# First layer of a four-layer fp32 model on one core: rows transposed between the tiles of the first projection block, retention worked off chunk by chunk between the tiles of the last four blocks

## The reference

```python
hn = rmsnorm(h, norm_gain[i])                       # rows of x
z = einsum('bsd,df->bsf', hn, w_in)                 # 1024 x 4096
qa, ka, va, ga, qb, kb, vb, gb = split(z, 8)        # 512 columns each
o_a = retention(qa, ka, va, ret_gn_gain)            # 4 heads of 128, chunks of 128 rows
o_b = stick_breaking(qb, kb, vb)                    # 4 heads of 128
mixed = concat([o_a * silu(ga), o_b * silu(gb)])
h = h + mixed @ w_out

# retention, for chunk n: q, k rotated by cos and sin of the position
scores = (qc @ kc.T) * intra
out = scores @ vc + (qc * qdec) @ state             # state: what the chunks before left
state = state * chunk_decay + (kc * kdec).T @ vc
o_a = head_norm(out) * gn_gain
```

## Time and profile before

| | us |
|---|---|
| median of 3 runs | 4376.22 |
| lowest, highest run | 4370.87, 4381.23 |
| the profiled execution | 4367.83 |
| its span | 4366.0 |
| PE busy in the span | 3796.1 (87%) |
| DVE busy | 2018.5 (46%) |
| ACT busy | 1699.4 (39%) |
| POOL busy | 103.8 (2%) |

### The profile page before, as it was taken

How to read it: one execution, slowest core, us unless ns; L and a number is a source line. 1 busy time by engine, 2 the same in 40 slices (tenths; PEclk the granted TensorE clock), 3 DMA queues, 4 the chain that set the end, 5 groups by cost and what they waited for, 6 DMA issues and landing times. The chain is left out here.

```text
span 4366.0 us, 48176 instructions
## 1 busy us (share of the span) xinstructions
PE 3796.1 (87%) x18874; PEld 3067.0 (70%) x18874; DVE 2018.5 (46%) x3947; ACT 1699.4 (39%) x3121; POOL 103.8 (2%) x120
## 2 busy tenths in 40 slices
PE   5998567998999599999789799999878999998789
PEld 4886533766887477777677677777766688887666
DVE  2111723235332567667524355555554355555442
ACT  3211156144342234333314344444433455555420
POOL 0000221000000000000000000000000000000000
PEclk9999778998999577777899899999978999999789
DMA  2222120221222111211222111011032011110310
GB/s 103 103 87 106 56 79 0 78 92 53 106 83 94 46 51 42 51 45 49 83 78 77 42 30 30 25 30 30 26 111 73 36 57 39 34 35 15 125 54 39
DMA packets 214841, 261.16 MB, mean 60 GB/s; under 512 B 62556, under 2 KB 138452, under 8 KB 213592
## 3 DMA queue, kind: packets, MB, share of 16 engines
q1 hardware_dynamic: 214616, 258.08, 18.0%
HBM read 189.60 MB, written 68.42 MB: 59 GB/s over the span
## 5 line engine op out<-in xcount | busy, mean ns | idle before, releaser
L301 PE MATMUL bank<-wh,XH 128*128 128x512 f32 x1344 | 556.1, 414 | 53.5 <-DVE wl L285 36.1
L301 PE MATMUL bank<-wl,XH 128*128 128x512 f32 x1344 | 532.1, 396 | 0.0
L301 PE MATMUL bank<-wh,XL 128*128 128x512 f32 x1344 | 531.6, 396 | 0.0
L2220 PE MATMUL bank<-XH,wh 128*128 128x512 f32 x1040 | 427.6, 411 | 32.0 <-DVE wl L2209 19.7
L2220 PE MATMUL bank<-XH,wl 128*128 128x512 f32 x1040 | 412.4, 397 | 0.0
L2220 PE MATMUL bank<-XL,wh 128*128 128x512 f32 x1040 | 411.6, 396 | 0.0
L301 PEld LDWEIGHTS bank<-wh,XH 128*128 128x128 f32 x1344 | 257.0, 191 | 125.3 <-issue 50.7
L285 DVE TENSOR_TENSOR wl<-raw,wh 128x1024 fp32r<-128x1024 f32 x128 | 153.9, 1224 | 407.8 <-ACT wh L279 406.6
L301 PEld LDWEIGHTS bank<-wh,XL 128*128 128x128 f32 x1344 | 256.9, 191 | 63.4 <-issue 10.3
L301 PEld LDWEIGHTS bank<-wl,XH 128*128 128x128 f32 x1344 | 256.0, 190 | 57.9
L301 PE MATMUL bank<-XH,wh 128*128 128x512 f32 x704 | 278.4, 395 | 6.0 <-DVE XL L1330 6.0
(11 more groups left out here) (398 smaller groups left out, 7314.3 us busy)
## 6 DMA issues: line engine op xcount, KB each, us to landing
sc_zt<-stage SPq DMA_DIRECT2D x88, 256.0 KB, 2.0
raw<-in_att_w_in SPq DMA_DIRECT2D x33, 512.0 KB, 4.2
raw<-in_even_w_in SPq DMA_DIRECT2D x32, 512.0 KB, 4.8
raw<-in_odd_w_in SPq DMA_DIRECT2D x32, 512.0 KB, 4.7
raw<-in_rec_w_in SPq DMA_DIRECT2D x32, 512.0 KB, 4.0
sc_h<-H SPq DMA_DIRECT2D x24, 512.0 KB, 2.6
H<-sc_h SPq DMA_DIRECT2D x24, 512.0 KB, 8.1
sc_z<-stage SPq DMA_DIRECT2D x40, 256.0 KB, 2.0
```

Of the source, the lines that this page charges most:

```text
L301: done = e.matmul(out, lhsT, rhs, start=k == 0 and j == 0, stop=k == NK - 1 and j == 2)
L2220: done = e.matmul(bank[:, :], x[:, k, :], y[:, k, ts], start=k == 0 and j == 0, stop=k == NK - 1 and j == 2)
```

## The change: what it does, and the diff

- `Start` is gone. `EvenIn` now carries one list, `plan`, that gives the order of all work for all engines: entries that stand in front of tile t, then tile t. Rows 0 and 1 are transposed ahead of it, row s (2 to 7) in front of tile s - 2, the squares of rows 3, 4 in front of tile 1 and of rows 5 to 7 in front of tile 3. The parts of the first weight block stand between rows 0, 1 and 2; those of block i + 1 in front of tiles 2 to 5 of block i.
- Tiles use two PSUM banks in turn (4 and 5) in place of eight; banks 0 to 3 take the transposes, then retention's.
- `Retention` has no phase of its own. Chunk n is read in front of tile 26 + 4n, rotated at 29 + 4n, transposed at 30 + 4n, scored at 31 + 4n, summed and normalized at 32 + 4n, and its result transposed at 34 + 4n.
- q is multiplied by its decay ahead of the matmul (`qd`, a table `qrow` in place of `qdec`), so both parts of the output accumulate in one bank; ScalarE copies it out. Most buffers exist once, z twice.
- The result goes to DRAM (rows 2048 to 2559 of `zt`) in place of `XH`, `XL`; `Stick` reads it back as `kept` and splits it on VectorE (`ve_kept`) four times, between its parts 1 and 2 at key blocks 5 to 2 of the first half.
- `Stick` does not wait for the last stores before its tables, q, k and v. SP reaches those loads after the last tile's store.

```diff
+    def plan(self):
+        order = [("sq", 0, 1), ("turn", 0), ("w", 0, 0), ("w", 0, 1), ("sq", 1, 3), ("turn", 1), ("w", 0, 2), ("w", 0, 3)]
+        front = {t: [] for t in range(64)}
+        for s in range(2, NS):
+            front[s - 2] += [("sq", *g) for g in self.GROUPS[2:] if g[0] == s] + [("turn", s)]
+        front[6] += [("features", 0)]
+        for t in range(56):
+            if 2 <= t % 8 <= 5:
+                front[t] += [("w", t // 8 + 1, t % 8 - 2)]
+        for n in range(NS):
+            for part, at in (("in", 26), ("rotate", 29), ("turn", 30), ("score", 31), ("sum", 32), ("out", 34)):
+                front[at + 4 * n] += [(part, n, "ret")]
+        for t in range(64):
+            order += front[t] + [("tile", t)]
+        return order
...
+    def sp(self, e, before, following):
...
+        for s in range(NS):
+            e.dma_start(self.rows[s][:, :], self.x[s * P:(s + 1) * P, :]).then_inc(*self.row[s].up())
+            if s == 0:
+                for q in range(3):
+                    self.w.load(e, q)
+            if s == 2:
+                self.w.load(e, 3)
...
+    def pe_tile(self, e, t):
+        i, j = t // 8, t % 8
+        if t >= 2:
+            f, k = self.out(t - 2)
+            e.wait_ge(*f.at(*k))
+        if i == 0:
+            wait_all(e, self.marks[j])
+        bank = self.c.banks[4 + t % 2]
...
+    def ac(self, e, before):
...
+            elif what == "sq":
+                for s in range(n, rest[0]):
...
+                    e.activation(self.sq[:, :], self.rows[s][:, :], ACT.Square, accum_out=self.st[:, s:s + 1]) \
+                        .then_inc(*self.squared.up(s))
+                e.wait_ge(*self.meant.at(n))
+                e.activation(self.st[:, n:rest[0]], self.st[:, n:rest[0]], ACT.Sqrt).then_inc(*self.rooted.up(n))
...
+            elif what == "tile":
+                e.wait_ge(*self.tile.at(n // 8, n % 8))
+                if n >= 4:
+                    e.wait_ge(*self.sent[n % 4].at(n - 4))
+                fn = ACT.Sigmoid if self.blocks[n // 8][2] else ACT.Copy
+                e.activation(self.stage[n % 4][:, :], c.banks[4 + n % 2][:, :], fn).then_inc(*self.copied.up(n))
...
 class Retention:
...
+    def pe(self, e, part, n):
...
+        if part == "turn":
+            e.wait_ge(*self.rotated.at(n))
...
+        elif part == "sum":
+            e.wait_ge(*self.masked.at(n))
+            if n:
+                e.wait_ge(*self.ocopied.at(n - 1))
+                e.wait_ge(*self.qdec.at(n))
+                e.wait_ge(*self.stated.at(n - 1))
+            for h in range(4):
+                if n:
+                    e.matmul(c.banks[3][:, hs(h)], self.qd[:, hs(h)], self.state[:, h, :], start=True, stop=False)
+                done = e.matmul(c.banks[3][:, hs(h)], self.sc[:, hs(h)], v[:, h, :], start=n == 0, stop=True)
+            done.then_inc(*self.summed.up(n))
...
+        elif part == "sum":
+            e.wait_ge(*self.summed.at(n))
+            if n:
+                e.wait_ge(*self.norm.at(n - 1))
+            e.activation(self.o[:, :], c.banks[3][:, :], ACT.Copy).then_inc(*self.ocopied.up(n))
+            e.wait_ge(*self.norm.at("var", n))
+            e.activation(self.mv[:, :, 1], self.mv[:, :, 1], ACT.Sqrt).then_inc(*self.rooted.up(n))
...
+    def po(self, e, n):
...
+        e.wait_ge(*self.zin[n % 2].at(n))
+        if n:
+            e.wait_ge(*self.rotated.at(n - 1))
+        e.tensor_tensor(B[:, :, 0, :], qk[:, :, 1, :], sin, ALU.mult)
+        e.tensor_tensor(B[:, :, 1, :], qk[:, :, 0, :], sin, ALU.mult).then_inc(*self.sines.up(n))
+        if n:
+            e.wait_ge(*self.gated.at(n - 1))
+        e.tensor_tensor(self.sg[:, :], z[:, 1536:2048], self.gn[:, :], ALU.mult).then_inc(*self.gains.up(n))
...
 class Stick:
...
     def sp(self, e, before):
-        wait_all(e, before)
+        wait_all(e, self.even_in.ret.read)
+        wait_all(e, [(self.even_in.sent[u % 4], (u,)) for u in range(52, 56)])
...
+        wait_all(e, before)
+        for h in range(4):
+            e.dma_start(self.kept[h][:, :], self.zt[2048 + h * P:2048 + (h + 1) * P, :]).then_inc(*self.keptin[h].up())
...
+    def ve_kept(self, e, h):
+        c = self.c
+        e.wait_ge(*self.keptin[h].at())
+        e.tensor_copy(c.XH[:, h, :], self.kept[h][:, :]).then_inc(*self.keph.up(h))
+        e.wait_ge(*self.keph.at(h))
+        e.tensor_tensor(c.XL[:, h, :], self.kept[h][:, :], f32(c.XH[:, h, :]), ALU.subtract).then_inc(*self.kepl.up(h))
...
+                if half == 1 and h == 3 and 2 <= kb <= 5:
+                    self.ve_kept(e, 5 - kb)
```

More of the change, by code:

```diff
@@ L302, in product @@
     return done
[L305 to L387, removed]
@@ L756, in po @@
         pass
[L759 to L767, removed]
-                                   for blk, mode, at in order], 4)
-        self.w = Weights(c, column_blocks(w_in), self.project.tile, 7, ahead=0)
-        self.marks, self.ends = self.start.marks, [(self.project.tile, (7, 7)), *self.project.stored]
-    def sp(self, e, before, following):
-        self.start.sp(e)
-        self.features.sp(e)
-        self.w.sp(e, 0)
-        sp_blocks(e, self.project, self.w, 8)
-        following.first(e)
-    def pe(self, e, before):
-        self.start.pe(e)
-        self.features.pe(e)
-        free = [[(self.start.low, (6 + j // 2, j % 2))] if j < 4 else [] for j in range(7)] + [[(self.features.copied, ())]]
-        pe_blocks(e, self.project, self.w, 8, [self.marks[j] + free[j] for j in range(8)])
-    def ac(self, e, before):
-        self.start.ac(e, self.w)
-        ac_blocks(e, self.project, self.w, 8)
-    def ve(self, e, before):
-        self.start.ve(e, self.w)
-        self.features.ve(e)
-        ve_blocks(e, self.project, self.w, 8)
-    def po(self, e, before):
-        pass
 def seq_rows(z, at):
@@ L904, in pe @@
                 for h in range(4):
[L905 to L906 removed]
+                    done = e.transpose(c.banks[j][:, hs(h)], self.A[:, 512 * j + P * h:512 * j + P * (h + 1)], c.ident[:, :])
+                done.then_inc(*self.turned.up(n, j))
+        elif part == "score":
+            e.wait_ge(*self.qk.at(n, 1))
+            if n:
+                e.wait_ge(*self.masked.at(n - 1))
+            for h in range(4):
+                done = e.matmul(c.banks[2][:, hs(h)], k(h), q(h), start=True, stop=True)
+            done.then_inc(*self.scored.up(n))
+            if n < NS - 1:
+                e.wait_ge(*self.decayed.at(n))
@@ L907, in pe @@
                 if n:
-                    for h in range(4):
-                        done = e.matmul(c.banks[4][:, hs(h)], q(h), self.state[:, h, :], start=True, stop=True)
-                    done.then_inc(*self.inter.up(n))
-                e.wait_ge(*self.decayed.at(n))
+                    e.wait_ge(*self.stated.at(n - 1))
                 for h in range(4):
-                    done = e.matmul(c.banks[5][:, hs(h)], self.heads(self.kd, n)[:, h, :], v[:, h, :], start=True, stop=True)
+                    done = e.matmul(c.banks[6][:, hs(h)], self.heads(self.kd)[:, h, :], v[:, h, :], start=True, stop=True)
@@ L914, in pe @@
                 done.then_inc(*self.kv.up(n))
-                e.wait_ge(*self.masked.at(n))
-                for h in range(4):
-                    done = e.matmul(c.banks[3][:, hs(h)], self.sc[n % 3][:, hs(h)], v[:, h, :], start=True, stop=True)
-                done.then_inc(*self.summed.up(n))
-            elif part == 3:
-                e.wait_ge(*self.gated.at(n))
-                for h in range(4):
-                    done = e.transpose(c.banks[6 + n % 2][:, hs(h)], self.y[n % 3][:, hs(h)], c.ident[:, :])
-                done.then_inc(*self.yturned.up(n))
@@ L3203, in program @@
         c.without_x()
-        both = [ret.marks[s] + stick.marks[s] for s in range(NS)]
         def sync(e):
             even_in.sp(e, [], end0.w)
-            ret.sp(e, even_in.ends)
-            stick.sp(e, ret.ends)
+            stick.sp(e, even_in.ends)
             end0.sp(e, stick.ends, odd_in)
```

442 lines of the change are left out of this document (279 added, 163 removed).

## The result

The changed kernel takes 4253.64 us (median of 4 runs, 4247.65 to 4270.02) against 4378.54 for the kernel before on the same chip (4 runs, 4370.87 to 4381.23): ratio 0.9723, 95% interval 0.9693 to 0.9754, faster by 124.9 us. The profiled execution took 4255.36, its span is 4253.6. The forecast was 4282 with a range of 4258 to 4318: direction and mechanism hold, the gain came out larger than the range allows.

The account below looks back on a forecast made before the run. Engine chains around a PE-bound product were taken as the bound. 30.2 + 359.0 + 19.7 + 37.4 + 4 + 11.6 gave stick-breaking's start at 461.9, not 557.70; less 1, a gain of 94.8 us: 4282, range 4258 to 4318.

Parts of the forecast that it names:

- The bound: Before stick-breaking: chains over several engines bind 60.65 us ahead of the product and 138.05 behind; PE alone binds the product.
- The start: Rows ahead of the product: first tile begins at 30.2 in place of 60.65; net gain about 10.8 us.
- Rival (c): Start doesn't come forward, through late weights or longer stops for squares: price 10.8 us, time about 4292, chance 0.05.
- What the product pays: Rows between the first tiles: two PE stops of 5.2 and 6.4 us, restarts, transposes and features, 19.7 us in all.
- Retention between the tiles: Eight chunks put 37.4 us of PE work into the product's stream, plus 4 us of waits for even chunks' rotations.
- Rival (b): Retention's chain stays in part, PE waiting in most chunks: price up to 43 us, time 4300 to 4325, chance 0.16.
- rival (d): Stops between the last 32 tiles pull PE to the 1.2 GHz level: slower, up to 4461, chance 0.04.
- Fewer banks, SP's queue: In the product, two tile banks and the reads and stores moved onto SP cost 0.
- The pause: Between the last tile and stick-breaking's first matmul PE pauses 11.6 us, as SP loads only behind the last store.
- Stick-breaking: Reading retention's result back and splitting it on DVE four times adds 1 us, bounds 0 and 9.6.
- 359.0: The product's 64 tiles by themselves take 359.0 us, as in the kernel before.
- (a): The forecast itself: 4266 to 4300, with 0 to 20 us of waits in place of 4; chance 0.74.

Follow-up runs that it names:

- The second series of the changed kernel: The changed kernel measured once more, unaltered, on one chip beside the kernel before: 4263.44 us (5 runs), ratio to before 0.9770.
- the kernel with both edits: Changed kernel with squares of rows 3 to 7 earlier and stick-breaking's loads ahead of tile 61's store: 4240.28 us, second time 4236.88.
- the earlier squares: Changed kernel with squares of rows 3, 4 ahead of tile 0 and of rows 5 to 7 ahead of tile 1: 4251.29 us.
- before with 128 bytes: Kernel before with tile `st` taking 128 bytes a partition in place of 32, moving the first projection's weights: 4376.64 us (one run).
- the one with the loads alone: Changed kernel with stick-breaking's tables and q, k, v of heads 0 to 2 issued ahead of tile 61's store: 4244.3 us.

## Why the prediction was right, and where it wasn't

**The bound** was named rightly. All the gain to stick-breaking's first matmul, 557.70 - 447.39 = 110.3 us (forecast 95.8), comes from the two stretches in which PE idled and from the pitch; what lies behind it changed by 2.1 us in sum.

**The start** held: 29.22 for 30.2, stops of 6.7 and 8.2 us with 11.1 of idle time for a forecast 11.6, and 10.2 net by the run that put the rows in front. Rival (c) falls.

**"What the product pays"** held in its sum. The transposes behind the first stop took 1.75, not 1.97.

**Retention between the tiles** held in its main term: 37.7 counted by insertions, 38.8 by the run with the rows first, for 37.4. Its small term was sized too high. The text put 1 us on each even chunk, since POOL's gate product would fall on the rotation. It ends before:

```profile
259.88 1.30 POOL L1062 TENSOR_TENSOR sg<-z,gn 128x512 f32<-128x512 f32 x1 [10.07 <-DVE y L1140]
...
262.44 0.69 DVE L1087 TENSOR_TENSOR A<-z,cos 128x512 f32<-128x512 f32 x1
...
264.37 0.69 DVE L1092 TENSOR_TENSOR A<-A,B 128x512 f32<-128x512 f32 x1
...
265.40 1.04 PE L990 MATMUL bank<-ident,A 128*128 128x128 f32 x8
```

POOL is done at 261.2, the rotation starts behind it at the short 0.69, ends at 265.06, and PE comes at 265.40. Counted from the end of tile 35 (252.27) that is 12.8 for the rotation and 13.1 for PE, where the forecast had 13.5 and 13.4: right to 0.7 us, with the sign on the good side, by a margin of 0.3. Rival (b), which saw PE waiting in most chunks, falls: PE waited 0.4 us, once. What those waits cost when they do come, the run with retention behind the product shows: 109 us.

**The clock**, rival (d), falls too. In the last 33 tiles, with 24 insertions, the granted clock is 1.00:

```profile
218.00:435.88 217.88, 217.88 (x1126) 185.48 (x1125) 89.44 (x218) 53.41 (x87) 30.92 (x21) 1.00 0.35 117
```

With retention behind the product its stretch has 0.59:

```profile
399.81:556.50 156.69, 71.34 (x337) 62.88 (x337) 79.00 (x204) 22.64 (x42) 35.99 (x28) 0.59 0.26 85
```

The Trainium skill (TensorE: Matmul & The Clock Gate, section A second HAM failure mode: psum-queue depth-cycling) tells of a bf16 kernel that cycles through PSUM banks and whose TensorE idles for moments between groups of matmuls. Here the two banks brought no such idling, 217.88 of 217.88 us busy, and no lower clock; the forecast took the banks alone for the cause.

**Fewer banks, SP's queue** cost nothing, as said: no wait of PE for a copy. **The pause** held, 11.51 for 11.6. **Stick-breaking** grew by 3.2 us to its last `q`k matmul, more than the 1 of the forecast and just over the 3 us that it named as a sign of being wrong; 1.5 of them are left at LayerEnd's first matmul. The bounds 0 and 9.6 hold. Its length scatters: 179.3 to 184.5 us in four profiles with the code of before in this phase, 182.6 to 187.8 in seven with that of after, on the mean 181.6 and 185.9. So a growth is likely. Whether it comes from the four splits on DVE or from the heads' later arrival (0.8 us more to the ninth matmul), no run tells.

**The step that failed** is the first term of the sum, "359.0". It took the product's length from before as fixed, because its instructions stayed the same. Their operands didn't stay where they were: with `Start` gone, `st` no longer lies in front of the weights. That is worth 9.9 us (359.0 - 349.1), shown by taking it away from after (+9.6) and giving it to before (-9.6). The trace of before held a sign of it. The same instruction (L301) had a pitch of 0.2267 in the unbroken stretch from 1100 to 1400 us, and 0.2333 in the first product, at a granted clock of 1.00 in both.

In the span the miss is 4271.2 - 4253.6 = 17.6 us: 1.0 from the start, 9.9 from the pitch, 3.6 from waits that didn't come (the small differences of the other terms cancel), and 3.1 behind stick-breaking's first matmul, where the forecast had 1 more and the trace 2.1 less. These 3.1 are within what the later stages scatter by. In the median it is 28.4, and the rest isn't the change's: 8.4 us were added because before's profiled execution lay below its median, after's lay 1.7 above its own, so 10.1, and 0.6 was rounding. The second series of the changed kernel has 4263.44 as its median, within the range: that the number fell outside it the first time, 4.4 us below, is decided by the scatter, the wrong first term is not. The low end of 4258 allowed for 4 us of waits and the runs, and had no room for a term of the product itself. The chances have a slip: (a) to (c) with half of (d) make 0.97, not 0.96.

## What to carry to other kernels

- An edit that takes tiles out or adds them moves all that is allocated behind them. Before taking the length of an untouched stretch over, compare its pitch with that of the same instruction elsewhere in the trace, and list the operands' addresses of both kernels.
- A chain over several engines is hidden when its parts stand between tiles of a stretch that PE fills: the same parts behind it cost 109 us more. What PE itself does in them can be counted from rows of such insertions to within one or two microseconds.
- Look behind the first late thing: the order of squares on ACT (12.5 us of the product) and the loads of the later heads on SP (9.3 us) were worth more in the trace than the pause that stood in the chain of waits (3.3 us). And see whether such a gain reaches the end: in the whole time of one series the squares brought 4 us on top of the loads.

## What the runs showed of the hardware

- **Pitch and place.** A matmul of 512 columns, 128 by 128 stationary, has a pitch of 0.2267 us in an unbroken stretch when its two SBUF operands lie a multiple of 256 bytes apart in the partition, and 0.2333 at 32 bytes beside that, whichever of the two (activations or weights) is the stationary one, with a granted clock of 1.00 either way. At 64 bytes 0.2289 or 0.2333, at 128 bytes 0.2333 or 0.2323, by block. Other distances weren't run. The mechanism is open.
- **Identical stages scatter.** From the last `q`k matmul of stick-breaking to a matmul early in `Fox`, its first of weights times v (line 2568 of after), all kernels run the same code (the end of `Stick`, `LayerEnd`, `OddIn`, `Rwkv`, `LayerEnd`, the beginning of `Fox`), and took 1771.7 to 1795.9 us. The windows of after and of the kernel with both edits:

```profile
635.00:2414.70 1779.70, 1575.91 (x8037) 1261.39 (x8036) 882.58 (x1765) 648.80 (x1160) 22.04 (x36) 0.87 0.21 66
```

```profile
603.80:2399.70 1795.90, 1593.48 (x8036) 1274.95 (x8035) 882.53 (x1765) 648.96 (x1160) 22.03 (x36) 0.86 0.21 65
```

DVE and ACT are busy for the same time, PE for 17.6 us more at a lower granted clock. So one span can't tell 20 us, and the positions up to stick-breaking's first matmul, which repeated within 2.3 us (product's end 435.88, 437.60 and 438.14), are what the readings above rest on. Whether the long times are tied to an edit is open: the three profiles with the earlier squares had 1789.4, 1793.0 and 1795.9, but the kernel with the rows first had 1792.8 and before with 128 bytes 1789.3, neither with that edit; the one with the loads alone had 1778.3. If a part is systematic, it gives back some of the 12.5 us of the squares.
